# First attention of a two-block transformer kernel: filling parts moved from its ninth phase to its compressed scores, low halves read from PSUM

## The chip, the cores and the metric

The kernel runs on one core of one Trainium2 chip. The metric is the device time of one execution in microseconds; the time of a kernel is the median of its runs. Five engines work side by side and meet only at semaphores: TensorE (PE in the profile; its weight loads are PEld), VectorE (DVE), ScalarE (ACT), GpSimd (POOL) and SyncE (SP), which issues the weight loads from memory. Each engine takes its own instructions strictly in their order.

## The reference

Two transformer blocks over 512 tokens of width 1024, in float32. The part around the change is the first block's attention (native sparse attention), in which 8 query heads in 2 groups of 64 channels look at compressed keys, selected blocks and a window:

```python
kc = compress(kv[0], cmp_pos_k[i], w_cmp_k1[i], w_cmp_k2[i])     # 31 compressed keys per group
vc = compress(kv[1], cmp_pos_v[i], w_cmp_v1[i], w_cmp_v2[i])
lc = jnp.einsum('bghqd,bgcd->bghqc', qb, kc)
pc = masked_softmax(lc, cmp_end[None, :] <= t[:, None])
o_c = jnp.einsum('bghqc,bgcd->bghqd', pc.astype(vc.dtype), vc)
...
o = gates[0] * o_c + gates[1] * o_s + gates[2] * o_w
y_a = o @ w_o_nsa[i]
c = causal_dwconv(c_val * jax.nn.sigmoid(c_gate), conv_w[i], conv_b[i])
c = jax.nn.silu(layernorm(c, conv_ln_g[i], conv_ln_b[i]))
y_b = c @ w_conv_out[i] + b_conv_out[i]
h = h + (ga * y_a + gb * y_b) @ w_out[i]
```

With 512 tokens there are 8 blocks of 64 keys, all of which are selected, so that both the selected and the window branch are causal attention over all earlier tokens, with keys and values of their own. The depthwise convolution has 31 taps over 512 channels, and the layernorm behind it takes its mean over these channels.

## The kernel before

Every float32 operand of TensorE is split into a high and a low half (`_hi`, `_lo`), and a product is three matmuls: high by high, low by high, high by low. A **unit** is one output tile of 128x512 accumulated over 8 blocks of 128 channels; a **part** is one eighth of it, three matmuls of 512 columns (L519 to L521). Weights come in slots of 128x1024: ScalarE makes `w_hi` (L1855) and GpSimd `w_lo` (L472). The high half of anything else is a copy on ScalarE (L1844), the low half a subtraction on VectorE (L1149).

The first attention stands between 124 and 343 us. It works on four pairs of heads. It has nine **phases** of four steps each, one step per query block (`j` and `i` in the code count them from 0; the text counts phases and steps from the first, pairs from 0 as the code does). The first, third, fifth and seventh phase make a pair's scores against the selected keys, the second, fourth, sixth and eighth those against the window's, and each phase turns and uses the probabilities of the phase before it: `turn` transposes a block of keys (L725), ScalarE and VectorE split it (`pt_hi`, `pt_lo`), `values` multiplies it with the values (L733). So the ninth phase has no scores, only transposes and values. Before the first phase and at the end of the second, fourth and sixth `cmp_scores(p)` makes the scores against the 31 compressed keys: two mask matmuls (L752) and 24 matmuls of 32 columns (L758).

Between these pieces TensorE does parts of 19 other units, the **filling parts**: three further query tiles and the 16 tiles of the merge gates, 152 parts. Their places are written out by hand in `NSA_FILL`: per step the parts after the scores, the parts at the step's end, and in the third, fifth, seventh and ninth phase a third number for the parts between the transposes and the values of the compressed branch. `nsa_made(j, i)` adds the table up; by it ScalarE and VectorE know in which step they scale or convert for a finished unit (`nsa_evict`). Eight parts stand outside the table behind it.

VectorE also does the 124 convolution taps (`taps`, L1206 and L1209): `EARLY_TAPS` of them before the attention, the others one or two a step until none is left. `LN_ADD` names the steps in which the finished channels are added up for the layernorm's mean; the ninth phase starts with a matmul of that sum (L816). Before the attention the compressed keys and values come out of PSUM bank 4 and 5 into `kc_f` and `vc_f`, ScalarE makes their high halves and VectorE their low ones:

```python
dve.tensor_copy(kc_f[0:HD, 0:NC1], ps[0:HD, 4, 0:NC1]).then_inc(s_cmp["out"], 1)
dve.tensor_copy(kc_f[HD:P, 0:NC1], ps[HD:P, 4, NC1:2 * NC1]).then_inc(s_cmp["out"], 1)
dve.tensor_tensor(vc_f[:], ps[0:2 * NC1, 5, 0:P], own[:], ALU.mult).then_inc(s_cmp["out"], 1)
...
low(kc_lo[:], kc_f[:], kc_hi[:], s_cmp["klo"])
low(vc_lo[:], vc_f[:], vc_hi[:], s_cmp["klo"])
```

TensorE waits for both (`s_cmp["klo"]`) before `cmp_scores(0)`.

## Time and profile before

| What | Value |
|---|---|
| Runs | 2183.87, 2184.62, 2186.61 us; median 2184.62 |
| Profiled execution | 2185.68 us, its span 2183.9 us |
| Mean granted TensorE clock | 0.994 of full speed |
| TensorE matmuls | busy 2146.1 us, 98% of the span, 10192 instructions |
| Weight loads of TensorE | busy 81% |
| VectorE, ScalarE, GpSimd | busy 46%, 40%, 43% |
| Chain that ended last | TensorE 89%, VectorE 6%, ScalarE 3%, nothing that the profile shows 1% |
| `w_hi` on ScalarE | 352 times, 1058 ns each |
| `w_lo` on GpSimd | 352 times, 2424 ns each |
| Part's three matmuls (128x512) | 391 to 399 ns each from start to end, overlapping |

A row of a timeline gives start, duration, engine, line, operation, output and inputs, and in square brackets how long the engine was idle before it and for whom. Matmuls are pipelined: their durations overlap, and what one costs is the distance from start to start. The kernel is one stream of matmuls with few gaps; other engines matter where TensorE waits for them.

### The profile page before, as it was taken

The page shows a single profiled execution, that of the slowest core. Times are in us where ns is not written, and L with a number is a line of the kernel's source. Part 1 is how long each engine was busy: PE and PEld are TensorE (multiplying, and loading weights), DVE is VectorE, ACT ScalarE, POOL GpSimd, SP SyncE. Part 2 cuts the span into 40 slices and gives each one's busy share as a digit, 9 for nine tenths or more (in the row PEclk, how much of TensorE's full clock was granted, in tenths as well). Part 3 has the DMA queues.
Part 4 walks back from the last instruction along what each step waited for, and adds up shares of the span by engine and source line. Part 5 has one row for each costly group of instructions (what it writes and reads, how often), then busy time and mean ns, then how long its engine had stood idle before and what let it go on. Part 6 is the DMA issues. An engine that isn't in the chain of part 4 may idle for free.

```text
span 2183.9 us, 25305 instructions
## 1 busy us (share of the span) xinstructions
PE 2146.1 (98%) x10192; PEld 1758.8 (81%) x10192; DVE 1013.6 (46%) x1637; ACT 869.6 (40%) x1358; POOL 933.8 (43%) x424
## 2 busy tenths in 40 slices
PE   9999999999999999999999999999999999999998
PEld 7877778888888887777778888888888888888886
...
DMA packets 53829, 193.27 MB, mean 88 GB/s; under 512 B 6096, under 2 KB 6224, under 8 KB 53712
## 3 DMA queue, kind: packets, MB, share of 16 engines
...
## 4 chain that ended last, share of the span: by engine, by line
PE 89%; DVE 6%; ACT 3%; issue 1%; DMA 0%; POOL 0%; DVEq 0%; ACTq 0%; POOLq 0%
PE ps L519 27%; PE ps L521 27%; PE ps L520 27%; PE ps L733 1%; DVE ps L1209 1%; PE ps L982 1%; PE ps L713 1%; PE ps L1000 1%; PE ps L725 1%; ACT w_hi L1855 1%; PE ps L615 1%; DVE xg_lo L1169 1%; PE ps L1007 0%; DVE ps L1730 0%; PE ps L715 0%
## 5 line engine op out<-in xcount | busy, mean ns | idle before, releaser
L472 POOL TENSOR_TENSOR w_lo<-w_raw,w_hi 128x1024 fp32r<-128x1024 f32 x352 | 852.6, 2424 | 1211.4 <-ACT w_hi L1855 1211.3
L519 PE MATMUL ps<-xg_hi,w_hi 128*128 128x512 f32 x1688 | 674.1, 399 | 5.4 <-POOL w_lo L486 2.8
L521 PE MATMUL ps<-xg_hi,w_lo 128*128 128x512 f32 x1688 | 661.2, 392 | 0.0
L520 PE MATMUL ps<-xg_lo,w_hi 128*128 128x512 f32 x1688 | 660.7, 391 | 0.0
L1855 ACT ACTIVATE w_hi<-w_raw 128x1024 fp32r<-128x1024 f32 x352 | 372.3, 1058 | 626.5 <-PE ps L521 623.8
L519 PEld LDWEIGHTS ps<-xg_hi,w_hi 128*128 128x128 f32 x1688 | 318.8, 189 | 69.3 <-issue 3.0
L521 PEld LDWEIGHTS ps<-xg_hi,w_lo 128*128 128x128 f32 x1688 | 318.5, 189 | 67.9
L520 PEld LDWEIGHTS ps<-xg_lo,w_hi 128*128 128x128 f32 x1688 | 319.2, 189 | 59.4
L521 PE MATMUL ps<-h_hi,w_lo 128*128 128x512 f32 x688 | 267.8, 389 | 0.0
L519 PE MATMUL ps<-h_hi,w_hi 128*128 128x512 f32 x688 | 267.8, 389 | 0.0
L520 PE MATMUL ps<-h_lo,w_hi 128*128 128x512 f32 x688 | 267.8, 389 | 0.0
L1143 DVE TENSOR_TENSOR ps<-ps,inv_rms 128x512 f32<-128x512 f32 x164 | 113.6, 696 | 194.2 <-PE ps L521 181.1
L521 PEld LDWEIGHTS ps<-h_hi,w_lo 128*128 128x128 f32 x688 | 129.2, 188 | 26.9
L520 PEld LDWEIGHTS ps<-h_lo,w_hi 128*128 128x128 f32 x688 | 129.2, 188 | 26.7
L519 PEld LDWEIGHTS ps<-h_hi,w_hi 128*128 128x128 f32 x688 | 129.2, 188 | 26.6
L1499 DVE TENSOR_TENSOR mixed<-mixed,ps 128x512 f32<-128x512 f32 x48 | 33.0, 688 | 199.9 <-PE ps L521 199.9
L1169 DVE SCALAR_TENSOR_TENSOR xg_lo<-resid,vec,xg_hi 128x512 fp32r<-128x512 f32 x72 | 85.5, 1191 | 12.7 <-ACT xg_hi L1881 12.5
L1209 DVE SCALAR_TENSOR_TENSOR ps<-glu,vec,ps 128x512 f32<-128x512 f32 x116 | 87.1, 751 | 1.9
L1844 ACT ACTIVATE h_hi<-ps 128x512 fp32r<-128x512 f32 x86 | 51.5, 598 | 90.1 <-DVE ps L1761 48.8
L1881 ACT ACTIVATE xg_hi<-resid,vec 128x512 fp32r<-128x512 f32 x72 | 51.7, 717 | 62.7 <-DVE resid L1499 40.2
L481 POOL TENSOR_TENSOR sq_sum<-sq_sum,sq 128x512 f32<-128x512 f32 x42 | 66.2, 1577 | 23.7 <-ACT sq L1878 21.4
L1761 DVE TENSOR_TENSOR ps<-tile_b,ps 128x512 f32<-128x512 f32 x64 | 44.6, 696 | 57.7 <-ACT tile_b L2296 57.7
...
## 6 DMA issues: line engine op xcount, KB each, us to landing
w_raw<-in_weights SPq DMA_DIRECT2D x352, 512.0 KB, 3.5
...
```

The costliest lines, as they stand in the source:

```text
L472: pool.tensor_tensor(w_lo[:, slot, :], w_raw[:, u % RAW, :], w_hi[:, slot, :].bitcast(F32), ALU.subtract).then_inc(w_ready, 1)
L481: pool.tensor_tensor(sq_sum[:], sq_sum[:], sq[:, m % 2:m % 2 + 1, :], ALU.add).then_inc(summed, 1)
L519: pe.matmul(o, w, x, start=start, stop=False)
L520: pe.matmul(o, w, xl, start=False, stop=False)
L521: return pe.matmul(o, wl, x, start=False, stop=stop)
L1143: dve.tensor_tensor(out, ps[:, BANK[u]:BANK[u] + 1, :], R[:], ALU.mult).then_inc(done, 1)
L1169: dve.scalar_tensor_tensor(xg_lo[:, m:m + 1, :], X[:, m:m + 1, :], g, xg_hi[:, m:m + 1, :].bitcast(F32), ALU.mult, ALU.subtract).then_inc( ...
L1209: ins = dve.scalar_tensor_tensor(acc if k < CONV_TAPS - 1 else conv_acc[:, ct, :], src, w, acc, ALU.mult, ALU.add)
L1761: dve.tensor_tensor(t, T2[:, m % 2:m % 2 + 1, :], t, ALU.mult).then_inc(s_mlp["s"], 1)
L1844: act.activation(out, x, ACT.Copy, scale=scale).then_inc(done, 1)
L1855: act.activation(w_hi[:, u % RING, :], w_raw[:, u % RAW, :], ACT.Copy).then_inc(w_hi_ready, 1)
L1881: act.activation(xg_hi[:, m:m + 1, :], X[:, m:m + 1, :], ACT.Copy, scale=g).then_inc(prep_hi, 1)
```

## The change

- `NSA_FILL` and three calls: three parts stand before TensorE's waits for the compressed halves, one inside `cmp_scores(0)`, between the second and the third query block, and two behind it; one part stands inside each later `cmp_scores`. The first phase thus holds 20 parts for 16, the second, fourth and sixth 17, the ninth 9 for 16.
- VectorE makes 64 taps before the attention (62 before), then one a step in the first phase and two a step in the second to the eighth; `cmp_normalise` moves in the first phase from its second step to its fourth; the first sum of channels moves from the first phase's second step to the third phase's third.
- `kc_f` and `vc_f` are gone. The product with `own` is written back into PSUM; high and low halves are made from PSUM, those of the keys in two pieces of 64x31. Two tiny instructions put zeros in the last column of `kc_hi` and `kc_lo` in place of the memset of `kc_f`.

```diff
--- before.py
+++ after.py
@@ -164,10 +164,11 @@
 
 
 MIX_CONV = {0: 2, 1: 3, 4: 5}
-EARLY_TAPS = 62
+EARLY_TAPS = 64
 EARLY_IDLE = 8
-LN_ADD = ((0, 1), (4, 0), (7, 3))
-NSA_FILL = [((2, 2),) * 4] + [((2, 2),) * 4, ((2, 2, 2), (2, 1), (2, 2), (2, 1))] * 4
+LN_ADD = ((2, 2), (4, 0), (7, 3))
+NSA_FILL = [((6, 2), (2, 2), (2, 2), (2, 2))] + [((2, 2), (2, 2), (2, 2), (2, 2, 1)), ((2, 2, 2), (2, 1), (2, 2), (2, 1))] * 3 + [
+    ((2, 2), (2, 2), (2, 2), (2, 2, 0)), ((2, 1, 1), (1, 1), (1, 1), (1, 0))]
 
 
 def nsa_made(j, i):
@@ -276,10 +277,8 @@
             kk_lo = sb("kk_lo", [P, 2, S], F32R, att)
             vv_hi = sb("vv_hi", [P, 2, 2, QB, P], F32R, att)
             vv_lo = sb("vv_lo", [P, 2, 2, QB, P], F32R, att)
-            kc_f = sb("kc_f", [P, NCP], scope=att)
             kc_hi = sb("kc_hi", [P, NCP], F32R, att)
             kc_lo = sb("kc_lo", [P, NCP], F32R, att)
-            vc_f = sb("vc_f", [2 * NC1, P], scope=att)
             vc_hi = sb("vc_hi", [2 * NC1, P], F32R, att)
             vc_lo = sb("vc_lo", [2 * NC1, P], F32R, att)
             gates = sb("gates", [P, QB, 32], scope=att)
@@ -743,7 +742,7 @@
                     part(u0 + at // DC, at % DC, at % DC + 1)
                 made[0] += n
 
-            def cmp_scores(p):
+            def cmp_scores(p, between):
 
                 pe.wait_ge(bank_free, query_unit(p) + 1)
                 if p:
@@ -757,6 +756,8 @@
                             rows = slice(hd * HD, (hd + 1) * HD)
                             mm = pe.matmul(ps[:, 2 + hd, qi * NCP:(qi + 1) * NCP], q[rows, p % 2, qs], k[rows, :],
                                            start=False, stop=t == 2 and qi == QB - 1)
+                    if qi < QB - 1 and between[qi]:
+                        fill(between[qi])
                 mm.then_inc(s_cs["scores"], 1)
 
             def cmp_turn(p):
@@ -793,18 +794,19 @@
                     pe.wait_ge(A1["olo"], b // 2)
                 head_values(A1, event(b) + kb, kb, vv_hi[:, :, b % 2], vv_lo[:, :, b % 2], b % 2 == 0 and kb == 0, b % 2 == 1 and kb == QB - 1)
 
+            fill(3)
             pe.wait_ge(c_act, 5)
             pe.wait_ge(s_kv["lo"], 6)
             pe.wait_ge(s_kv["zero"], 4)
-            pe.wait_ge(s_cmp["klo"], 2)
+            pe.wait_ge(s_cmp["klo"], 4)
             for j in range(9):
                 b = j - 1
                 for i in range(QB):
                     pieces = NSA_FILL[j][i]
                     if j < 8:
                         if j == 0 and i == 0:
-                            cmp_scores(0)
-                            fill(pieces[0])
+                            cmp_scores(0, (0, 1, 0))
+                            fill(2)
                         scores(j, i)
                     if j or i:
                         fill(pieces[0])
@@ -825,7 +827,9 @@
                                 cmp_values(b // 2)
                         turn(b, i)
                     if j % 2 and i == QB - 1 and j < 7:
-                        cmp_scores(j // 2 + 1)
+                        cmp_scores(j // 2 + 1, (0, pieces[2], 0))
+                    elif j == 7 and i == QB - 1:
+                        fill(pieces[2])
                     fill(pieces[1])
             fill(4)
             values(7, QB - 1)
@@ -1261,7 +1265,8 @@
                 dve.wait_ge(unit_done, uu + 1)
                 dve.tensor_tensor(kv_dup[0:HD, j, :], ps[0:HD, BANK[uu], :], R[0:HD, 0, :], ALU.mult).then_inc(s_cmp["dup"], 1)
                 dve.tensor_tensor(kv_dup[HD:P, j, 0:S - 1], ps[HD:P, BANK[uu], 1:S], R[HD:P, 0, 1:S], ALU.mult).then_inc(bank_free, 1)
-            dve.memset(kc_f[:], 0.0).then_inc(s_cmp["out"], 1)
+            for t in (kc_hi, kc_lo):
+                dve.tensor_scalar(t[:, NC1:NCP], ones[:, 0:1], 0.0, None, ALU.mult).then_inc(s_cmp["out"], 1)
             dve.wait_ge(s_cmp["dup"], 4)
             dve.wait_ge(bank_free, U["cmp_in"] + 4)
             blocks(0, "pos_k")
@@ -1303,15 +1308,14 @@
             query_low(0)
             values_low(1)
             dve.wait_ge(unit_done, U["cmp_out"] + 1)
-            dve.wait_ge(s_cmp["out"], 1)
-            dve.tensor_copy(kc_f[0:HD, 0:NC1], ps[0:HD, 4, 0:NC1]).then_inc(s_cmp["out"], 1)
-            dve.tensor_copy(kc_f[HD:P, 0:NC1], ps[HD:P, 4, NC1:2 * NC1]).then_inc(s_cmp["out"], 1)
-            dve.tensor_tensor(vc_f[:], ps[0:2 * NC1, 5, 0:P], own[:], ALU.mult).then_inc(s_cmp["out"], 1)
+            dve.tensor_tensor(ps[0:2 * NC1, 5, 0:P], ps[0:2 * NC1, 5, 0:P], own[:], ALU.mult).then_inc(s_cmp["out"], 1)
             dve.memset(token[:, 12:13], 0.0).then_inc(bank_free, 1)
             dve.wait_ge(s_cmp["khi"], 2)
-            dve.wait_ge(s_cmp["out"], 4)
-            low(kc_lo[:], kc_f[:], kc_hi[:], s_cmp["klo"])
-            low(vc_lo[:], vc_f[:], vc_hi[:], s_cmp["klo"])
+            for g in range(2):
+                rows = slice(g * HD, (g + 1) * HD)
+                low(kc_lo[rows, 0:NC1], ps[rows, 4, g * NC1:(g + 1) * NC1], kc_hi[rows, 0:NC1], s_cmp["klo"])
+            dve.wait_ge(s_cmp["khi"], 3)
+            dve.tensor_tensor(vc_lo[:], ps[0:2 * NC1, 5, 0:P], vc_hi[:].bitcast(F32), ALU.subtract).then_inc(s_cmp["klo"], 2)
             dve.wait_ge(s_kv["lo"], 2)
             scaled(U["gates"], T[:, 0:1, :])
 
@@ -1435,9 +1439,9 @@
                             dve.tensor_copy(gates[:], ps[:, 4, 0:QB * 32].rearrange("p (a b) -> p a b", b=32)).then_inc(s_gate["ready"], 1)
                             dve.wait_ge(s_gate["ready"], 1)
                     nsa_evict(nsa_made(j, i - 1) if i else nsa_made(j - 1, QB - 1) if j else 0)
-                    if tapped[0] < CT * CONV_TAPS:
+                    if j and tapped[0] < CT * CONV_TAPS:
                         taps(1)
-                    if i == 1 and br == 0 and j < 8:
+                    if i == (1 if j else QB - 1) and br == 0 and j < 8:
                         cmp_normalise(p)
                     if j < 8:
                         head_normalise(A1, QB * j + i, i, stat, (prob_s, prob_w)[br],
@@ -1979,9 +1983,12 @@
             query_high(0)
             values_high(1)
             highs(U["cmp_out"] + 1 + RING)
-            act.wait_ge(s_cmp["out"], 4)
-            copy_hi(kc_hi[:], kc_f[:], s_cmp["khi"])
-            copy_hi(vc_hi[:], vc_f[:], s_cmp["khi"])
+            act.wait_ge(unit_done, U["cmp_out"] + 1)
+            for g in range(2):
+                rows = slice(g * HD, (g + 1) * HD)
+                copy_hi(kc_hi[rows, 0:NC1], ps[rows, 4, g * NC1:(g + 1) * NC1], s_cmp["khi"])
+            act.wait_ge(s_cmp["out"], 3)
+            copy_hi(vc_hi[:], ps[0:2 * NC1, 5, 0:P], s_cmp["khi"])
             highs(U["gates"] + 1 + RING)
             taken(U["gates"])
             act.activation(ln_sum[:], T[:, 0, :], ACT.Sigmoid).then_inc(s_gate["sig"], 1)
```

**TensorE, at the first compressed scores.** `cmp_mask_r` is the mask, `kc` the compressed keys, `xg` the normed input of the filling parts. Before:

```order
L520 MATMUL ps<-xg_lo,w_hi 128x512
L521 MATMUL ps<-xg_hi,w_lo 128x512
L752 MATMUL ps<-cmp_mask_r,ident_r 128x128 x2
L758 MATMUL ps<-kc_hi,q_hi 128x32 x2
L758 MATMUL ps<-kc_lo,q_hi 128x32 x2
L758 MATMUL ps<-kc_hi,q_lo 128x32 x2
L758 MATMUL ps<-kc_hi,q_hi 128x32 x2
L758 MATMUL ps<-kc_lo,q_hi 128x32 x2
L758 MATMUL ps<-kc_hi,q_lo 128x32 x2
L758 MATMUL ps<-kc_hi,q_hi 128x32 x2
L758 MATMUL ps<-kc_lo,q_hi 128x32 x2
```

After (the two rows ahead of the mask end the three new filling parts):

```order
L519 MATMUL ps<-xg_lo,w_hi 128x512
L520 MATMUL ps<-xg_hi,w_lo 128x512
L751 MATMUL ps<-cmp_mask_r,ident_r 128x128 x2
L757 MATMUL ps<-kc_hi,q_hi 128x32 x2
L757 MATMUL ps<-kc_lo,q_hi 128x32 x2
L757 MATMUL ps<-kc_hi,q_lo 128x32 x2
L757 MATMUL ps<-kc_hi,q_hi 128x32 x2
L757 MATMUL ps<-kc_lo,q_hi 128x32 x2
L757 MATMUL ps<-kc_hi,q_lo 128x32 x2
L518 MATMUL ps<-xg_hi,w_hi 128x512
L519 MATMUL ps<-xg_lo,w_hi 128x512
L520 MATMUL ps<-xg_hi,w_lo 128x512
```

The first query blocks' small matmuls now stand between filling parts; before, all 24 stood in a row behind the gates' unit, whose rows read like filling parts.

**VectorE, from the query's scaling to the gates' scaling**, ahead of the same scores. `vv` are values, `token` a one-column dummy. Before:

```order
L1143 TENSOR_TENSOR ps<-ps,inv_rms 128x512
L1297 SCALAR_TENSOR_TENSOR q_lo<-ps,q_hi 128x512
L1149 TENSOR_TENSOR vv_lo<-ps,vv_hi 128x4x64 x2
L1307 COPY kc_f<-ps 64x31
L1308 COPY kc_f<-ps 64x31
L1309 TENSOR_TENSOR vc_f<-ps,own 62x128
L1310 MEMSET token 128x1
L1149 TENSOR_TENSOR kc_lo<-kc_f,kc_hi 128x32
L1149 TENSOR_TENSOR vc_lo<-vc_f,vc_hi 62x128
L1143 TENSOR_TENSOR tile_a<-ps,inv_rms 128x512
```

After:

```order
L1213 SCALAR_TENSOR_TENSOR ps<-glu,vec,ps 128x512
L1147 TENSOR_TENSOR ps<-ps,inv_rms 128x512
L1302 SCALAR_TENSOR_TENSOR q_lo<-ps,q_hi 128x512
L1153 TENSOR_TENSOR vv_lo<-ps,vv_hi 128x4x64 x2
L1311 TENSOR_TENSOR ps<-ps,own 62x128
L1312 MEMSET token 128x1
L1153 TENSOR_TENSOR kc_lo<-ps,kc_hi 64x31 x2
L1318 TENSOR_TENSOR vc_lo<-ps,vc_hi 62x128
L1147 TENSOR_TENSOR tile_a<-ps,inv_rms 128x512
L1382 TENSOR_REDUCE c_stat<-ps 128x8
```

The copies into `kc_f` are gone, the product stays in `ps`, and the low halves read `ps`.

**Ninth phase, TensorE between the second transposes and their values.** Before:

```order
L725 MATMUL ps<-ident,prob_w 128x128 x6
L519 MATMUL ps<-xg_hi,w_hi 128x512
L520 MATMUL ps<-xg_lo,w_hi 128x512
L521 MATMUL ps<-xg_hi,w_lo 128x512
L519 MATMUL ps<-xg_hi,w_hi 128x512
L520 MATMUL ps<-xg_lo,w_hi 128x512
L521 MATMUL ps<-xg_hi,w_lo 128x512
L519 MATMUL ps<-xg_hi,w_hi 128x512
L520 MATMUL ps<-xg_lo,w_hi 128x512
L521 MATMUL ps<-xg_hi,w_lo 128x512
L733 MATMUL ps<-pt_hi,vv_hi 128x384
```

After:

```order
L724 MATMUL ps<-ident,prob_w 128x128 x6
L518 MATMUL ps<-xg_hi,w_hi 128x512
L519 MATMUL ps<-xg_lo,w_hi 128x512
L520 MATMUL ps<-xg_hi,w_lo 128x512
L518 MATMUL ps<-xg_hi,w_hi 128x512
L519 MATMUL ps<-xg_lo,w_hi 128x512
L520 MATMUL ps<-xg_hi,w_lo 128x512
L732 MATMUL ps<-pt_hi,vv_hi 128x384
```

One of three parts is gone here. **ScalarE in the same phase**, from the compressed branch's high half to the sigmoids (`sq` are the layernorm's squares). Before:

```order
L1855 ACTIVATE w_hi<-w_raw 128x1024
L1844 ACTIVATE pt_hi<-ps 62x512
L1844 ACTIVATE pt_hi<-ps 128x1024
L2060 ACTIVATE sq<-conv_acc 128x512 x2
L1844 ACTIVATE pt_hi<-ps 128x2x384
L2060 ACTIVATE sq<-conv_acc 128x512 x2
L1855 ACTIVATE w_hi<-w_raw 128x1024
L1844 ACTIVATE pt_hi<-ps 128x2x256
L2037 ACT_TABLE_LOAD
```

After:

```order
L1859 ACTIVATE w_hi<-w_raw 128x1024
L1848 ACTIVATE pt_hi<-ps 128x2x128
L1848 ACTIVATE pt_hi<-ps 62x512
L1848 ACTIVATE pt_hi<-ps 128x1024
L2067 ACTIVATE sq<-conv_acc 128x512 x2
L1859 ACTIVATE w_hi<-w_raw 128x1024
L1848 ACTIVATE pt_hi<-ps 128x2x384
L2067 ACTIVATE sq<-conv_acc 128x512 x2
L1848 ACTIVATE pt_hi<-ps 128x2x256
```

Each `w_hi` stands one step earlier: the first ahead of the small high halves, the second ahead of the high half of 128x2x384 instead of behind it.

## Rows read from the trace of the kernel before

**Rows 1.** Waits of TensorE, 40 to 350 us: total us, times, longest us.
```profile
PE ps L752 <- DVE vc_lo L1149: 4.1, 1, 4.1
PE ps L752 <- ACT prob_w L2001: 1.6, 3, 0.5
PE ps L713 <- ACT prob_s L2001: 0.7, 2, 0.4
```

**Rows 2.** Windows: us, PE, PEld, DVE, ACT, POOL busy (count), clock, DMA share, GB/s.
```profile
128.00:142.00 14.00, 14.00 (x70) 10.84 (x69) 6.20 (x17) 4.15 (x11) 0.00 (x0) 0.63 0.10 40
170.00:177.00 7.00, 6.48 (x46) 5.02 (x45) 3.12 (x8) 1.48 (x6) 0.00 (x0) 0.76 0.15 55
219.00:226.00 7.00, 6.55 (x57) 5.62 (x57) 5.16 (x13) 2.74 (x9) 0.00 (x0) 1.00 0.09 32
266.00:273.00 7.00, 6.51 (x44) 5.20 (x45) 3.68 (x10) 1.22 (x5) 0.00 (x0) 0.76 0.09 35
500.00:790.00 290.00, 290.00 (x1281) 240.24 (x1280) 118.92 (x168) 106.19 (x135) 132.54 (x55) 1.00 0.31 100
```

**Rows 3.** Timeline of TensorE: first mask, two filling parts slow, and two at full clock.
```profile
127.83 0.41 PE L752 MATMUL ps<-cmp_mask_r,ident_r 128*128 128x128 f32 x2 [4.06 <-DVE vc_lo L1149]
...
130.74 0.79 PE L519 MATMUL ps<-xg_hi,w_hi 128*128 128x512 f32 x1
...
133.59 0.47 PE L713 MATMUL ps<-kk_hi,q_hi 64*128 64x128 f32 x2
...
221.23 0.50 PE L519 MATMUL ps<-xg_hi,w_hi 128*128 128x512 f32 x1
...
222.81 0.33 PE L713 MATMUL ps<-kk_hi,q_hi 64*128 64x128 f32 x2
```

**Rows 4.** Timeline of VectorE before the first mask.
```profile
115.25 3.92 DVE L1209 SCALAR_TENSOR_TENSOR ps<-glu,vec,ps 128x512 f32<-128x512 f32 x5
...
122.93 0.28 DVE L1309 TENSOR_TENSOR vc_f<-ps,own 62x128 f32<-62x128 f32 x1
...
123.71 1.48 DVE L1149 TENSOR_TENSOR kc_lo<-kc_f,kc_hi 128x32 fp32r<-128x32 f32 x1 [0.49 <-ACT vc_hi L1844]
125.11 2.47 DVE L1149 TENSOR_TENSOR vc_lo<-vc_f,vc_hi 62x128 fp32r<-62x128 f32 x1
```

**Rows 5.** Timeline of GpSimd, the same stretch.
```profile
122.77 4.67 POOL L472 TENSOR_TENSOR w_lo<-w_raw,w_hi 128x1024 fp32r<-128x1024 f32 x2 [2.34 <-ACT w_hi L1855]
```

**Rows 6.** Timelines of VectorE, ScalarE and TensorE, end of the third phase.
```profile
195.84 1.23 DVE L1339 TENSOR_REDUCE stat<-ps 128x2 f32<-128x1024 f32 x1
...
197.78 0.68 ACT L2001 ACTIVATE prob_s<-ps,stat 128x512 f32<-128x512 f32 x1
...
198.80 0.33 PE L713 MATMUL ps<-kk_hi,q_hi 64*128 64x128 f32 x2
```

**Rows 7.** Timeline of VectorE, end of the eighth phase: the last sum for the mean.
```profile
316.28 0.68 DVE L1415 TENSOR_TENSOR ln_sum<-ln_sum,conv_acc 128x512 f32<-128x512 f32 x1
```

**Rows 8.** Timeline of TensorE, ninth phase: eight transposes, then each step's first values.
```profile
321.49 1.09 PE L725 MATMUL ps<-ident,prob_w 128*128 128x128 f32 x8
...
325.17 0.40 PE L733 MATMUL ps<-pt_hi,vv_hi 128*128 128x512 f32 x1
...
329.27 0.43 PE L733 MATMUL ps<-pt_hi,vv_hi 128*128 128x384 f32 x1
...
333.60 0.28 PE L733 MATMUL ps<-pt_hi,vv_hi 128*128 128x256 f32 x1
...
338.30 0.33 PE L733 MATMUL ps<-pt_hi,vv_hi 128*128 128x128 f32 x1 [0.17 <-DVE pt_lo L1149]
```

**Rows 9.** Timeline of VectorE, ninth phase: low half of the eight transposes.
```profile
323.68 1.22 DVE L1149 TENSOR_TENSOR pt_lo<-ps,pt_hi 128x1024 fp32r<-128x1024 f32 x1 [3.13 <-ACT pt_hi L1844]
```

**Rows 10.** Timeline of ScalarE, ninth phase: the two sigmoids.
```profile
333.81 3.72 ACT L2037 ACTIVATE merge<-merge 128x2048 f32<-128x2048 f32 x2
```

**Rows 11.** Timeline of TensorE behind the last values of the second attention.
```profile
1114.78 0.79 PE L519 MATMUL ps<-fo_hi,w_hi 128*128 128x512 f32 x1 [1.41 <-DVE fo_lo L1149]
```

## The prediction

> **What bounds the kernel now.** I read the waits of TensorE first. The page's table says that TensorE is busy nearly all of the span, so that only three things can change the time: waits of TensorE, stretches in which it runs at a lower clock, and work taken from it. The change takes no work from TensorE (the same filling parts, elsewhere), so the first two are the whole account. The waits view of the stretch 40 to 350 us [rows 1] shows where the first attention waits: 4.1 us once, before the mask that opens the scores against the compressed keys, for VectorE's `vc_lo`; 0.7 us in two waits for `prob_s` in the first phase; 1.6 us in three waits for `prob_w` (0.52 each, before the compressed scores of the pairs 1 to 3). Then the granted clock by windows [rows 2]: 0.63 over the 14 us behind the long wait, that is 14 x 0.37 = 5.2 us of clock lost; 0.76 over 7 us at 170 and again at 266 us (1.7 us each), both right behind a 0.52 us wait and the 24 matmuls of 32 columns; and 1.00 at 219 us, where the same instructions stand behind the same wait. The two levels of the clock are 2.4 and 1.2 GHz: two filling parts took 1.58 us at the one and 2.85 us at the other [rows 3], a ratio of 1.8 where the clock's is 2. So of lost clock I count 0.92: 4.8 us in front, 1.6 us for each later fall.
>
> The third view is VectorE's timeline before the long wait [rows 4]: `kc_lo`, 128x32, took 1.48 us and `vc_lo`, 62x128, took 2.47 us, while the product `vc_f`, as small but read from PSUM, took 0.28. GpSimd ran two `w_lo` from 122.77 to 127.44 us [rows 5]; these two low halves read both operands from SBUF and the second ends within 0.2 us of GpSimd's. They waited for GpSimd, not for arithmetic.
>
> **The change, part by part.**
>
> *Low halves from PSUM.* The two copies into `kc_f` go (0.43 us up to the product's start), `kc_lo` becomes two short pieces and `vc_lo` one, all with one operand in PSUM. Two more taps stand ahead: five took 3.92 us, so 1.57 us [rows 4]. VectorE's product moves from 122.93 to 122.93 - 0.43 + 1.57 = 124.07 us and ends at 124.3. From the product's end to `kc_lo` it took 0.55 us before over ScalarE's high halves; ScalarE no longer waits for VectorE with `kc_hi`, so this is a bound from above: 124.85. Then 0.2 + 0.2 + 0.28 = 0.7 us give 125.5 in place of 127.6. The bounds: if the pieces cost nothing 124.9, if one of them still waits for a `w_lo` (end at 125.1 or 127.4) 127.6. I take 125.5, since every PSUM operand beside that `w_lo` ran at its short time.
>
> The Trainium skill, page "VectorE: DVE Perf Modes", section "Rules for kernel authors", advises for elementwise work on a matmul's output to accept the PSUM rate or "copy PSUM→SBUF first if you'll do many ops", which is what the kernel before does. By that rule the change would lose here; by the rows above it gains, since the copied operands were those that took long.
>
> *Three parts before the scores.* TensorE was done with the gates' unit at 127.83 - 4.06 = 123.8 us [rows 3]. A part is three matmuls of 512 columns; 1281 of mostly such matmuls took 290 us [rows 2], 0.226 each, so 0.68 a part. Three parts last until 125.8, just past 125.5. The wait of 4.1 us shrinks to about 0.1: **-4.0**. These parts need the weights of the first pair unit, converted long before. What was late next is TensorE's own queue.
>
> *The clock in front.* With no idle ahead of it and a part between the second and the third query block's small matmuls, the stretch starts at full clock: **-4.8**, between 0 (it falls all the same) and -5.2.
>
> *VectorE's first phase.* Four taps, one running sum and the compressed normalisation leave its first two steps. Its peaks then come as the scores do, and the two waits for `prob_s` go: **-0.7**. The last step carries the normalisation, 1.5 us more, but TensorE's next scores wait for the exponentials of the step's scores, which precede it.
>
> *One part inside the compressed scores of pairs 1 to 3.* It stands behind the 0.52 us wait and covers none of it, so its only worth is the clock. The same rows fell at two places and not at a third, so one part may or may not tip it. I take one of the two falls as gone, **-1.6**, between -3.2 and +1.6 (a fall at the third place too).
>
> *The counts shift.* With four more parts in the first phase, units end one step earlier or later afterwards, and so do the scaling on VectorE (0.69) and the `w_hi` on ScalarE (1.06). In the third phase VectorE's second step now holds a `merge` scaling and its third the moved sum into `ln_sum`: the peak of the fourth query block moves from 195.84 to about 196.6 us. ScalarE's exponentials ended at 198.46 and TensorE's next scores began at 198.80 without a wait [rows 6]; the slack of 0.3 is less than the shift, so a wait of some 0.6 appears. In the seventh phase a scaling and a `w_hi` in its third step do the same for 0.5. **+1.1**, between 0 (TensorE's other work hides it) and +2.
>
> *The ninth phase.* It loses seven of 16 parts, 4.8 us of work. Was it cover? First, the mean's matmul waits for the third sum into `ln_sum`. Before, the last tap fell a step earlier; now tap and sum stand at the end of the eighth phase. The sum ran at 316.28 for 0.68 us [rows 7] and the tap adds 0.78, with a `w_hi` on ScalarE ahead of the high half: the matmul that stood at 317.0 starts 0.9 us later. Then the chain transposes, high half on ScalarE, low half on VectorE, values. The eight transposes began at 321.49 and their values at 325.17 [rows 8]; the low half between them ran from 323.68 for 1.22 us [rows 9], so the values could have begun at 324.95: slack 0.2, where two parts (1.4 us) go. At the following values, 329.27, slack is nil. The last ones, at 338.30, waited 0.17 us, because ScalarE was in the two sigmoids of 128x2048 (3.72 us from 333.81) [rows 10]. The steps between values were 4.10, 4.33 and 4.70 us. Without the parts they are set by the chain: 4.6 (a `w_hi` now comes before the high half), 3.2 (that `w_hi` of 1.06 us is gone from here) and 5.0 (table load, sigmoids, high and low half in a row). So the phase ends 0.2 + 1.1 - 0.5 - 0.3 = 0.5 us sooner than before from a start 0.9 us late: with 4.8 us of work gone it is 0.4 us longer, and **+5.2** is what the parts taken away cost here as idle. Bounds +4.2 and +6.2.
>
> *The clock in the ninth phase.* Its end is now 1.4 us idle, six matmuls of 128 columns and four of one column. The nearest row is at 1114.78 us: a wait of 1.41 us behind small matmuls, and the next 512-column matmul takes 0.79 us, as long as the one at 130.74 and not 0.50 like the one at 221.23, so the clock is at its lower level [rows 3, 11]. I take one fall, priced like those at 170 and 266 us before the 0.92: **+1.7**, between 0 and +3.4.
>
> The Trainium skill, page "TensorE: Matmul & The Clock Gate", section "Why this matters for your kernels", says that it takes a long gap between bursts of matmuls to lose the clock. By that rule none of the ninth phase's short waits would cost a fall; the falls at 170 and 266 us, behind 0.52 us, contradict it. It is the first rival below.
>
> Sum: -4.0 - 4.8 - 0.7 - 1.6 + 1.1 + 5.2 + 1.7 = -3.1. The profiled execution took 2185.68 us (its span 2183.9 and 1.8 around it) and would come to 2182.6; it stands 1.06 above the median of the three runs, and from that median of 2184.62 the forecast is 2181.5.
>
> **The rivals.**
>
> *The clock holds in the ninth phase.* The waits there are split by full matmuls, unlike at 1114 us. Then the last term is 0: -4.8, 2179.8; with both later falls gone too -6.4, 2178.2. For it: 219 us, no fall. Against: both sides of the last wait are small matmuls.
>
> *More is late behind.* All three places fall, or ScalarE's and VectorE's shifted work adds waits elsewhere: 1.6 to 4 us on top, -1.5 to +1, 2183.1 to 2185.6.
>
> *The front doesn't do what it says.* `vc_lo` comes at 127 us after all, TensorE idles 1 us and the clock falls as before: -3.1 + 4.8 + 1.0 = +2.7, 2187.3. Against: the PSUM rows.
>
> *The ninth phase at half clock, slower than before.* From the transposes at 321.49 to the values at 338.30 stand 16.8 us; less 0.2 idle and six parts (4.1) 12.5 us of work remain. At half clock they take 12.5 x 1.8 = 22.5, which passes the chain's 16.3 by 6.2; the tail behind adds 1.7. With -4.8 for the rest and the later falls kept (+1.6): +4.7, 2189.3. It decides only if the clock falls at the first of the waits and stays down until the end, for some 17 us; half of that would end at no change. The long slow stretch in front lasted 10 us and had far less work in it.
>
> **How the numbers follow.** Forecast case 0.38; the clock holds in the ninth phase 0.36, nearly all of it below 2180.25; more is late 0.14; the front fails 0.05; the ninth phase at half clock 0.05; the rest, 0.02, lies on both sides. What a measurement of this kernel tells from no change is about 0.2%, 4.4 us: faster means below 2180.25, slower above 2189.0. So faster 0.35 (the first rival without its upper edge), same 0.59, slower 0.06. The range that holds 8 in 10 runs from the better end of the first rival with a little measured spread, 2177.7, to the worse end of the second, 2185.5.
>
> **What would show it.** Right: no wait before the first mask above 0.3 us; clock 1.00 from 128 to 142 us; `kc_lo` and `vc_lo` at or below 0.3 us; waits of 0.9, 1.0, 1.2, 1.3, 0.4 and 1.4 us in the ninth phase, 5 to 6 us in all; waits of half a microsecond at the fourth phase's and the eighth's first scores; a slow stretch behind the ninth phase's last values. Wrong: ninth-phase waits of under 4 us (then a link of the chain that I took as fixed was itself driven by TensorE), a wait for `vc_lo`, or a clock that differs from this at the four places.

## The result, and the profile after

The changed kernel took 2195.30 us (median of 6 runs, 2191.54 to 2196.53) against 2186.05 for the kernel before in the same comparison: a ratio of 1.0042 with a 95% interval of 1.0032 to 1.0053, 9.2 us slower. I had forecast 2181.5 with a range up to 2185.5, and slower than before with a chance of 0.06. The forecast was wrong, in sign and by more than its range.

The profiled execution took 2196.53 us, its span 2194.8 (before 2183.9). The waits of TensorE, 40 to 360 us, which answer to [rows 1] (total us, times, longest us; line numbers are those of each kernel's own file):

```profile
PE ps L732 <- DVE pt_lo L1153: 7.5, 7, 1.8
PE ps L712 <- ACT prob_s L2008: 1.9, 3, 0.9
PE ps L818 <- DVE ln_sum L1419: 1.7, 1, 1.7
PE ps L751 <- ACT prob_w L2008: 1.6, 3, 0.5
PE ps L724 <- DVE prob_s L1351: 1.4, 1, 1.4
PE ps L772 <- DVE pt_lo L1153: 0.7, 1, 0.7
```

The wait of 4.1 us for `vc_lo` is gone, as forecast. But 6.6 us of waits (those of [rows 1] and the 0.2 of [rows 8]) have become 14.8. The windows, which answer to [rows 2] (us, busy us and count of PE, PEld, DVE, ACT and POOL, granted clock, DMA share, GB/s):

```profile
128.00:142.00 14.00, 14.00 (x85) 10.16 (x84) 8.74 (x20) 6.62 (x17) 4.15 (x2) 1.00 0.32 96
170.00:177.00 7.00, 7.00 (x35) 5.41 (x34) 2.67 (x7) 1.82 (x6) 0.00 (x0) 0.77 0.22 75
217.00:228.00 11.00, 10.48 (x70) 8.30 (x69) 6.08 (x14) 3.98 (x12) 2.44 (x1) 0.84 0.15 49
345.00:360.00 15.00, 14.37 (x67) 12.15 (x68) 7.19 (x13) 11.20 (x16) 4.78 (x2) 0.89 0.22 70
```

In front the clock is 1.00 for 0.63. Of the two later falls, at 170 and 266 us, the second is gone (1.00 from 262 to 275 us, where its mask now stands), and there is one at 222 us that was not there before. The one I expected behind the ninth phase is there. In front, the low halves read from PSUM are short although two `w_lo` run beside them (start us, us, engine, line, operation):

```profile
125.03 4.72 POOL L471 TENSOR_TENSOR w_lo<-w_raw,w_hi 128x1024 fp32r<-128x1024 f32 x2 [3.98 <-ACT w_hi L1859]
...
125.26 0.41 DVE L1153 TENSOR_TENSOR kc_lo<-ps,kc_hi 64x31 fp32r<-64x31 f32 x2 [0.17 <-ACT kc_hi L1848]
...
125.70 0.28 DVE L1318 TENSOR_TENSOR vc_lo<-ps,vc_hi 62x128 fp32r<-62x128 f32 x1
```

To see where the time goes I cut the attention at the four masks that open the compressed keys' scores, at the mean's matmul and at the matmul that spreads the normalisation behind the ninth phase. TensorE by these stages (us, busy us and count, granted clock, DMA share, GB/s), the kernel before:

```profile
127.83:170.94 43.11, 41.91 (x222) 0.88 0.15 49
170.94:219.45 48.51, 47.96 (x281) 0.96 0.13 45
219.45:266.49 47.04, 46.46 (x282) 1.00 0.13 45
266.49:317.02 50.53, 50.51 (x294) 0.97 0.15 44
317.02:342.74 25.72, 25.55 (x134) 1.00 0.13 41
```

and the changed kernel:

```profile
126.29:166.67 40.38, 38.48 (x227) 1.00 0.21 66
166.67:218.50 51.83, 49.29 (x284) 0.97 0.13 41
218.50:270.33 51.83, 49.22 (x284) 0.97 0.14 42
270.33:324.38 54.05, 50.50 (x296) 1.00 0.13 40
324.38:351.64 27.26, 23.07 (x112) 0.94 0.13 39
```

By the second mask the changed kernel is 4.3 us ahead; the three stages behind it lose 3.3, 4.8 and 3.5 us, though each has one filling part (three matmuls, 0.7 us) more. The ninth phase, 22 recorded matmuls shorter, takes 1.5 us longer. At its end the kernel is 8.9 us behind, of the 10.9 between the two spans and the 9.2 between the medians. The other 2.0 us come later, where the change edits nothing: the clock of this execution also falls at 1080, 1120 and 1760 us (0.83, 0.83 and 0.86 over 10 us each), that of the kernel before only at 1110 us (0.83). Within the attention, then, the middle stages lost what I had not priced. Their waits on TensorE's timeline (start us, us, in brackets the idle time before and who ended it):

```profile
148.82 1.09 PE L724 MATMUL ps<-ident,prob_s 128*128 128x128 f32 x8 [1.37 <-DVE prob_s L1351]
...
189.44 0.44 PE L732 MATMUL ps<-pt_hi,vv_hi 128*128 128x384 f32 x1 [1.14 <-DVE pt_lo L1153]
...
241.93 0.44 PE L732 MATMUL ps<-pt_hi,vv_hi 128*128 128x384 f32 x1 [1.79 <-DVE pt_lo L1153]
```

with a fourth of 1.08 us in the seventh phase. Ahead of each, VectorE and GpSimd (start us, us, engine, line, operation):

```profile
145.71 3.06 DVE L1351 TENSOR_SCALAR prob_s<-prob_s,stat,gates 128x512 f32<-128x512 f32 x2
...
146.09 2.39 POOL L471 TENSOR_TENSOR w_lo<-w_raw,w_hi 128x1024 fp32r<-128x1024 f32 x1 [6.49 <-ACT w_hi L1859]
...
184.99 2.41 POOL L471 TENSOR_TENSOR w_lo<-w_raw,w_hi 128x1024 fp32r<-128x1024 f32 x1 [14.99 <-ACT w_hi L1859]
...
185.16 2.51 DVE L1399 TENSOR_TENSOR prob_c<-prob_c,c_stat 128x248 f32<-128x248 f32 x1
```

The scaling of `prob_c` takes 2.51 us, and ends 0.27 us behind a `w_lo` that began 0.17 us before it. So do the other two in the fifth and seventh phase; only the one of the first phase is short. In the kernel before, the four of them took 0.42 each (duration ns min/median/max, first line the changed kernel, second the kernel before):

```profile
L1399 DVE TENSOR_TENSOR prob_c<-prob_c,c_stat x4: 416/2497/2506, 145.2 to 287.3; 128x248 f32<-128x248 f32 x4
...
L1395 DVE TENSOR_TENSOR prob_c<-prob_c,c_stat x4: 416/416/419, 141.9 to 283.4; 128x248 f32<-128x248 f32 x4
```

That is the same picture as `kc_lo` and `vc_lo` in front [rows 4, 5], which I had read as waits for GpSimd, and then had not looked for at the places to which the shifted counts move a `w_lo`. The Trainium skill, page "SBUF — State Buffer", section "SBUF: two separate sides", says that VectorE and GpSimd share a pair of ports that is locked for a whole instruction: an operation of VectorE with two SBUF inputs, or in one of its two-port modes, blocks until a GpSimd operation that began first has ended. The rows above agree for `prob_c`, which has two SBUF inputs, and so do the rows of the experiments. `prob_s` has one tensor input and waits as well, 3.06 us for 1.00; which mode it ran in no row shows.

The theory to test, the **collision theory**: the table's shifted counts bring ScalarE's `w_hi`, and with it GpSimd's `w_lo`, one step earlier, beside operations of VectorE that have all their tensors in SBUF. The rival, the **load theory**: VectorE simply has more work in these steps (a merge scaling of 0.68 us that also came one step earlier, the first phase's normalising), and the long duration is only a part of it.

### The profile page after: what moved, and what is told of

The parts are those of the page before. It is cut to its first block, busy times and chain, and to the rows that moved or that the text cites. A ratio compares the mean times of both kernels' runs of the same rounds, so it can differ in the third digit from the quotient of the medians.

```text
span 2194.8 us, 25305 instructions
## 1 busy us (share of the span) xinstructions
PE 2149.2 (98%) x10192; PEld 1758.7 (80%) x10192; DVE 1020.7 (47%) x1637; ACT 870.0 (40%) x1359; POOL 933.9 (43%) x424
## 4 chain that ended last, share of the span: by engine, by line
PE 89%; DVE 6%; ACT 3%; issue 1%; DMA 0%; POOL 0%; DVEq 0%; ACTq 0%; POOLq 0%
PE ps L518 27%; PE ps L520 27%; PE ps L519 27%; PE ps L986 1%; PE ps L1004 1%; PE ps L732 1%; PE ps L712 1%; DVE stat L1343 1%; ACT w_hi L1859 1%; PE ps L614 1%; PE ps L724 1%; DVE xg_lo L1173 1%; PE ps L1011 0%; DVE pt_lo L1153 0%; PE ps L1013 0%
## 5 line engine op out<-in xcount | busy, mean ns | idle before, releaser
L1162 DVE TENSOR_TENSOR sq_sum<-sq_sum,ps 128x512 f32<-128x512 f32 x57 | 39.1, 687 | 69.4 <-ACT ps L1876 69.1
```

Source lines behind the costliest of these rows:

```text
L1162: dve.tensor_tensor(sq_sum[:], sq_sum[:], ps[:, NB:NB + 1, :], ALU.add).then_inc(summed, 2 if m == DC - 2 and in_two_parts(n) else 1)
```

## The experiments

All medians are set against the kernel before on the same chip. Each kernel has one trace, of one execution; executions of one kernel differ in their mean granted clock (0.994 to 0.996 in the six of the changed kernel), so a single fall of the clock that a trace shows need not stand in the others.

| kernel | median, us | before, us | ratio, 95% interval |
|---|---|---|---|
| the change | 2195.30 | 2186.05 | 1.0042 (1.0032 to 1.0053) |
| high_late | 2190.05 | 2186.22 | 1.0020 (1.0010 to 1.0030) |
| scale_late | 2205.72 | 2186.22 | 1.0094 (1.0080 to 1.0108) |
| table_only | 2198.31 | 2186.22 | 1.0060 (1.0047 to 1.0072) |
| vector_only | 2189.46 | 2186.22 | 1.0018 (1.0009 to 1.0027) |
| mean_clear | 2182.82 | 2184.76 | 0.9993 (0.9985 to 1.0002) |
| vector_clear | 2183.95 | 2184.76 | 0.9998 (0.9989 to 1.0007) |
| ninth_thin | 2193.34 | 2184.76 | 1.0032 (1.0019 to 1.0044) |
| front_four | 2179.56 | 2184.76 | 0.9977 (0.9969 to 0.9986) |
| norm_late | 2191.20 | 2185.06 | 1.0030 (1.0020 to 1.0039) |
| part_behind | 2182.86 | 2185.06 | 0.9997 (0.9988 to 1.0006) |
| sum_early | 2178.16 | 2185.06 | 0.9971 (0.9960 to 0.9983) |
| first_thin | 2179.86 | 2185.06 | 0.9976 (0.9967 to 0.9985) |

### high_late: the w_lo back in its old steps

```diff
 # ScalarE; NSA_WAS is NSA_FILL of the kernel before
-                while counted[0] < n // DC:
+                while counted[0] < (n if at_query(counted[0]) or late is None else late) // DC:
...
-                    nsa_evict(nsa_made(j, i - 1) if i else nsa_made(j - 1, QB - 1) if j else 0)
+                    nsa_evict(nsa_made(j, i - 1) if i else nsa_made(j - 1, QB - 1) if j else 0,
+                              nsa_made(j, i - 1, NSA_WAS) if i else nsa_made(j - 1, QB - 1, NSA_WAS) if j else 0)
```

`at_query` picks the three query tiles among the units; they stay on the new counts, the merge tiles go back to the old ones.

> The changed kernel, with ScalarE alone back on the unit counts of before: a weight tile's rounding to w_hi, and so GpSimd's subtraction that makes w_lo from it, again begins in the third step of the odd phases and no longer in the second. Everything else, VectorE's scaling of the finished merge tiles included, stays on the shifted counts. Collision theory (GpSimd's w_lo of 2.4 us holds up VectorE's operations whose operands all lie in SBUF): VectorE's prob_c scaling falls from 2.5 to 0.42 us in the third, fifth and seventh phase, prob_s of the first phase's last step from 3.06 to 1.0 us, the waits of 1.37, 1.14, 1.79 and 1.08 us at TensorE shrink to 0.3 or less, and the time falls by 5 to 7 us against the changed kernel's 2195.3, to about 2189.5. Load theory (VectorE has simply too much in these steps: merge scaling and normalising together): the same waits, and 2195 +-1.

It came out 5.2 us faster than the changed kernel, at the near end of the forecast. The scaling of `prob_c`, and TensorE's waits:

```profile
L1406 DVE TENSOR_TENSOR prob_c<-prob_c,c_stat x4: 416/416/419, 144.2 to 280.5; 128x248 f32<-128x248 f32 x4
```

```profile
PE ps L739 <- DVE pt_lo L1160: 3.4, 4, 1.1
PE ps L825 <- DVE ln_sum L1426: 1.9, 1, 1.9
PE ps L719 <- ACT prob_s L2015: 1.9, 2, 1.2
```

All four waits of the middle stages are gone; the four for `pt_lo` that are left lie in the ninth phase. VectorE's merge scaling was in the same step as in the changed kernel, so its load there was not the cause by itself. Waits for `prob_s` at the third and fifth phase's end, and the mean's, are left.

### norm_late: the w_lo stays, the operation that it holds up goes elsewhere

```diff
-                    if i == (1 if j else QB - 1) and br == 0 and j < 8:
+                    if i == (2 if j else QB - 1) and br == 0 and j < 8:
                         cmp_normalise(p)
```

> The changed kernel, ScalarE's and GpSimd's work and all counts as they are; only VectorE's normalising of the compressed probabilities moves from the second to the third step of the odd phases, out of the way of the w_lo that stands in the second. Collision theory: prob_c takes 0.42 instead of 2.5 us, the three waits of 1.14, 1.79 and 1.08 us at TensorE go (the first phase's 1.37 and the mean's 1.72 stay), unless the third step, now 1.4 us fuller, makes others of some tenths: 3 to 4.5 us faster than the changed kernel's 2195.3, about 2191.5. Load theory: the same 1.4 us of small operations only move, and new waits of about a microsecond appear in the third step: 2195.

4.1 us faster than the changed kernel (3.1 when each is set against the kernel before in its own comparison): within the forecast, though nothing on ScalarE or GpSimd was moved. All four `prob_c` take 0.42 us, and the waits of 1.14, 1.79 and 1.08 us are gone. In the third phase the `w_lo` at 182.33 us now meets VectorE's low half and tap, which take one operand from PSUM, and neither is longer for it (before, 0.96 and 0.75 as well):

```profile
182.33 2.40 POOL L471 TENSOR_TENSOR w_lo<-w_raw,w_hi 128x1024 fp32r<-128x1024 f32 x1 [13.48 <-ACT w_hi L1859]
...
183.31 0.96 DVE L1153 TENSOR_TENSOR pt_lo<-ps,pt_hi 128x768 fp32r<-128x768 f32 x1 [0.96 <-ACT pt_hi L1848]
184.18 0.75 DVE L1213 SCALAR_TENSOR_TENSOR ps<-glu,vec,ps 128x512 f32<-128x512 f32 x1
```

In the third and fifth phase the 1.4 us of small operations did not turn into a wait in the third step. In the seventh there is one, and it is a collision again: a later `w_lo` meets `prob_s` (two of 128x384, 0.87 us otherwise), TensorE waits 0.74 us for the low half behind it and 1.38 us, for 0.73, at the phase's end.

```profile
284.95 2.62 POOL L471 TENSOR_TENSOR w_lo<-w_raw,w_hi 128x1024 fp32r<-128x1024 f32 x1 [3.42 <-ACT w_hi L1859]
...
285.44 2.74 DVE L1351 TENSOR_SCALAR prob_s<-prob_s,stat,gates 128x384 f32<-128x384 f32 x2
...
288.83 0.39 PE L732 MATMUL ps<-pt_hi,vv_hi 128*128 128x256 f32 x1 [0.74 <-DVE pt_lo L1153]
```

So 4.0 us of waits went and 1.0 came: 3.0 us net, and the clock falls behind that last wait (0.83 from 290 to 300 us) and no longer at the masks.

### scale_late: the merge scaling back, the w_lo stays

The same edit as high_late, in VectorE's loop in place of ScalarE's.

> The changed kernel, with VectorE alone back on the unit counts of before: its scaling of a merge tile (0.68 us) leaves the second step of the odd phases for the third, while ScalarE's w_hi and GpSimd's w_lo stay in the second. Load theory: each of the three waits in the odd phases falls by up to 0.7 us, about 2 us in all, to 2193. Collision theory: the w_lo still begins beside the prob_c scaling, which starts 0.6 us earlier and ends with the w_lo as before; waits and time stay, 2195 +-1 (a bank that comes free later could add some tenths).

Both expectations missed: the kernel is 10 us slower than the changed one. The first line of its waits says why, and it is a cost of the experiment's own: the filling parts wait for banks whose merge tiles are scaled too late.

```profile
PE ps L525 <- DVE merge L1154: 14.5, 7, 4.1
```

So its time tells nothing between the theories. Its trace does. With the 0.68 us of scaling out of the step, `prob_c` gets in ahead of the `w_lo` and takes 0.42; the operation behind it, `prob_s` (two of 128x256, 0.73 us otherwise), is held up in its place:

```profile
286.86 0.42 DVE L1406 TENSOR_TENSOR prob_c<-prob_c,c_stat 128x248 f32<-128x248 f32 x1
...
287.29 2.38 POOL L478 TENSOR_TENSOR w_lo<-w_raw,w_hi 128x1024 fp32r<-128x1024 f32 x1 [14.19 <-ACT w_hi L1867]
...
287.39 2.75 DVE L1358 TENSOR_SCALAR prob_s<-prob_s,stat,gates 128x256 f32<-128x256 f32 x2
```

Which operation pays was a matter of tenths of a microsecond here; an operation with only SBUF operands in the 2.4 us of the `w_lo` paid in both kernels.

### table_only and vector_only: the change in two halves

table_only is the kernel before with the edits to TensorE's order alone (`NSA_FILL`, the three parts in front, `between`); vector_only the kernel before with all the rest of the diff.

> The kernel before, with only what the change does to TensorE's order: three parts ahead of the first scores' waits, parts between the compressed keys' scores, the new table; VectorE and ScalarE as before (fp32 copies kc_f and vc_f, taps, first phase's normalising, additions in their old steps), but on the shifted unit counts. Collision theory: most of the loss is here; the first phase's prob_c scaling stands in its second step, away from a w_lo, so that the 3.06 us is gone, but the three 2.5 us are there: front gain of 4 to 6, less 4 to 5 of ninth phase, less 4 of collisions and their followers, less clock: about +5 to +8 against before, near 2192. If instead VectorE's own changes cost the time (taps out of the first phase, normalising in its fourth step): about 2183 to 2187 here.

> The kernel before, with only the edits to VectorE and ScalarE: low halves from PSUM, two taps earlier, no taps in the first phase, its normalising in the fourth step, the first addition in the third phase; TensorE's order and the unit counts as before. Collision theory: no collision in the odd phases; the front wait of 4.1 falls by some 1.6 us, the first phase's two waits of 0.7 us go: 2 to 3 us faster than before, 2183.5. If VectorE's own changes cost the time: 2188 or more.

table_only lost 12 us, more than the whole change, and 4 more than the most that I expected. Here the first phase's normalising was still in its second step, and I had thought it clear of a `w_lo` there. It is not: `prob_c` takes 2.5 us four times out of four, and in the first phase TensorE pays all of it.

```profile
L1401 DVE TENSOR_TENSOR prob_c<-prob_c,c_stat x4: 2493/2497/2499, 140.2 to 289.5; 128x248 f32<-128x248 f32 x4
```

```profile
147.00 0.53 PE L714 MATMUL ps<-kk_hi,q_hi 64*128 64x512 f32 x2 [3.12 <-ACT prob_s L2007]
```

Lost clock comes on top: 0.56 from 147 to 150 us, behind that wait, and 0.82 over the ninth phase (0.94 in the changed kernel).

vector_only was meant to gain 2 to 3 us and lost 3.2. (Its first phase has one tap a step left, not none as the expectation says.) Half of it behaved: the wait for `vc_lo` is 1.8 us for 4.1, the first phase's two waits are gone, and no `prob_c` is long. One wait of 0.83 us for `prob_s` came at the third phase's end. A loss that the trace explains sits at the mean. The last tap now falls at the end of the eighth phase, the third sum into `ln_sum` right behind it, and that sum has SBUF operands alone:

```profile
317.46 2.34 POOL L470 TENSOR_TENSOR w_lo<-w_raw,w_hi 128x1024 fp32r<-128x1024 f32 x1 [4.85 <-ACT w_hi L1855]
...
317.55 2.80 DVE L1415 TENSOR_TENSOR ln_sum<-ln_sum,conv_acc 128x512 f32<-128x512 f32 x1
...
320.40 2.08 PE L816 MATMUL ps<-ln_sum,mean_ch 128*128 128x512 f32 x2 [2.76 <-DVE ln_sum L1415]
```

The sum takes 2.80 for 0.68 us [rows 7], the mean's matmul waits 2.76, and it takes 2.08 us where it took 1.12 in the kernels before and after: the clock had fallen (0.94 over that last stage). The wait and that clock are some 4 us, and not the whole of what was lost against the gains in front. In this execution the stages between the second and the fourth mask are 2.6 and 3.1 us longer than in the kernel before, at a clock of 0.93 each for 0.96 and 1.00. Why it fell longer there, no experiment shows; the mean clock of the eleven executions goes from 0.990 to 0.995.

### mean_clear and vector_clear: that w_lo behind the sum

```diff
-                    nsa_evict(nsa_made(j, i - 1) if i else nsa_made(j - 1, QB - 1) if j else 0)
+                    if (j, i) != (8, 0):
+                        nsa_evict(nsa_made(j, i - 1) if i else nsa_made(j - 1, QB - 1) if j else 0)
...
                             cmp_high(b // 2)
+                            if j == 8:
+                                nsa_evict(nsa_made(j, i - 1) if i else nsa_made(j - 1, QB - 1) if j else 0)
```

on ScalarE, in high_late (there with the second limit too) and in vector_only (shown).

> high_late, and behind the eighth phase ScalarE rounds its weight tile only after the compressed values' high half, so that GpSimd's w_lo no longer runs beside VectorE's last addition into ln_sum, for which the mean's matmul waits. Collision theory: the addition takes 0.68 instead of 1.96 us, the mean's wait falls from 1.9 to about 0.7, and the time by 1.3 to 2 us, to 2188.5. Rival (the wait is the late last tap, and the addition's length does not matter): wait and time as in high_late, 2190.

> vector_only with the same edit to ScalarE. Collision theory: the addition falls from 2.80 to 0.68 us, the mean's wait from 2.8 to 0.7 or less, and the half clock on the mean's matmuls behind that wait (2.08 us for two) goes too: 3 to 4 us, to about 2186, the level of the kernel before or a little under it. Rival: VectorE's edits cost elsewhere (the later last tap, the waits at the third phase's first scores): 2189 stays.

In both the sum takes 0.69 us and the mean's wait is 0.65. The gains are 7.2 us between the medians of high_late and mean_clear and 5.5 between those of vector_only and vector_clear (5.8 and 4.0 when each is set against the kernel before of its own comparison). For mean_clear that is much more than the 1.3 to 2 that I forecast. The traces of high_late and mean_clear show 4.3 us of it by the end of the ninth phase: the shorter wait, and a clock of 1.00 in two stages where high_late had 0.97 (the third) and 0.94 (the ninth phase). Why the clock held there, once in a stage that the edit does not reach, no row says. For high_late the single runs lie 6.7 us apart, for mean_clear 3.1. What is shown of this edit is the sum's 0.69 us and the shorter wait, 1.3 us.

### ninth_thin: the ninth phase's parts as cover

The kernel before with the ninth phase's table of the change, and the seven parts behind it:

```diff
-NSA_FILL = [((2, 2),) * 4] + [((2, 2),) * 4, ((2, 2, 2), (2, 1), (2, 2), (2, 1))] * 4
+NSA_FILL = [((2, 2),) * 4] + [((2, 2),) * 4, ((2, 2, 2), (2, 1), (2, 2), (2, 1))] * 3 + [
+    ((2, 2),) * 4, ((2, 1, 1), (1, 1), (1, 1), (1, 0))]
...
             mm.then_inc(s_ln["var"], 1)
-            fill(4)
+            fill(11)
```

> The kernel before, with nothing but the ninth phase's table of the change: seven of its sixteen parts are taken out and stand behind it, in the second filling ahead of the wait for the normalisation's reciprocal, where TensorE has nothing to wait for. The same parts are computed in all. My term for the ninth phase: 7 x 0.68 = 4.8 us of cover lost, all of it turned to idle, plus 1.7 if the clock falls behind it: +5 to +6.5, to about 2192. If the parts were not needed as cover: 2186. If the gaps pull the clock down in the phase itself: 2196 or more.

8.6 us between the medians, interval 4.2 to 9.6, where I expected 5 to 6.5; the five executions lie in two groups, at 2188 and 2193.5. By the traces its last stage is 32.08 us for 25.72, 6.4 more with the same work. Idle is 4.0 us of that, 0.7 of it before the compressed branch's values:

```profile
PE ps L733 <- DVE pt_lo L1149: 3.5, 3, 2.0
```

```profile
338.00:346.00 8.00, 7.07 (x31) 0.79 0.22 66
```

and the clock, 0.79 over 8 us behind the last values, 1.7. In the trace my two terms for the ninth phase hold: the parts were cover, 4.0 of their full price of 4.8, and the fall comes on top. The 0.7 us that is left is in neither.

### front_four and part_behind: what a part between the compressed scores is worth

front_four is mean_clear with no part in the later phases' compressed scores and twelve in the ninth phase; part_behind is mean_clear with each of the three parts right behind those scores in place of between them.

```diff
-                        cmp_scores(j // 2 + 1, (0, pieces[2], 0))
+                        cmp_scores(j // 2 + 1, (0, 0, 0))
+                        fill(pieces[2])
```

> mean_clear, with only the four parts of the front kept: no part stands between the later phases' compressed scores, and the three parts that stood there are back in the ninth phase, twelve instead of nine. Against mean_clear three parts of cover come back, 2.0 us; the odd phases' first-scores waits change with the counts by some tenths. If the parts between the compressed scores bring nothing: 1.5 to 2.5 faster than mean_clear, 2186.5. If they hold the clock there (1.00 for 0.76 in a stretch of 7 us is 1.7 us each): mean_clear's time or up to 2 us more.

> mean_clear, with each of the three parts that stood between the compressed keys' scores of the later phases now right behind those scores: order alone, all counts equal. If the parts between hold the clock: a granted clock of 0.76 to 0.87 at one or two of these places and 1 to 3 us slower than mean_clear's 2182.8. If the clock there hangs on the waits before the masks and what came before them: equal, 2182.8 +-1.

In the trace of part_behind the clock does not need the part. Over the stretches with the 24 small matmuls:

```profile
164.00:172.00 8.00, 7.47 (x61) 1.00 0.08 33
213.00:221.00 8.00, 7.48 (x61) 1.00 0.10 39
261.00:270.00 9.00, 8.46 (x67) 1.00 0.00 0
```

And a part does not always protect it: in the changed kernel the fall at 222 us begins behind one.

```profile
219.61 0.50 PE L518 MATMUL ps<-xg_hi,w_hi 128*128 128x512 f32 x1
...
220.98 0.36 PE L757 MATMUL ps<-kc_lo,q_hi 64*128 64x32 f32 x2
...
221.48 0.79 PE L518 MATMUL ps<-xg_hi,w_hi 128*128 128x512 f32 x1
```

The medians of part_behind and mean_clear are equal, 2182.86 and 2182.82; its three stages are each 0.3 us shorter by the traces, which I take for the price of breaking the small matmuls up. The single executions leave a doubt: six of the eleven of part_behind had a mean clock of 0.995 or 0.996, up to 2187.20 us, all eleven of mean_clear 0.997 or 0.998, up to 2184.08. Whether the part helps in some executions is therefore open. It is not needed where none stands there or right behind: front_four and sum_early had 0.997 or 0.998 in all of their 17 executions. front_four, which gives three parts of cover back, is 3.3 us faster than mean_clear (I expected 1.5 to 2.5) and 5.2 faster than the kernel before, with an interval that leaves 1 out.

### sum_early and first_thin: what else can be had

```diff
-LN_ADD = ((2, 2), (4, 0), (7, 3))
+LN_ADD = ((2, 0), (4, 0), (7, 3))
```

first_thin also has `((6, 2), (2, 1), (2, 1), (1, 1))` for the first phase and the full sixteen parts in the ninth.

> front_four, with the first addition into ln_sum moved from the third phase's third step (where the trace of front_four shows it at 1.24 us beside the end of a w_lo, and TensorE waiting 1.20 us for prob_s four microseconds later) to its first step, where VectorE idles 3 us. Collision theory: that wait falls to 0.6 or less, 0.6 to 1.2 us faster than front_four's 2179.56, about 2178.7. If the wait belongs to the shifted counts alone: no change.

> sum_early, with the four parts of the front taken from the rest of the first phase (16 parts in all there again) and the ninth phase full at sixteen. The ninth phase's waits beyond the compressed values' (1.6 us) go; four parts less in the first phase either uncover VectorE there, up to 2.7 us of idle at its scores or first turn, or stay hidden since its taps are gone. If hidden: 1.5 us faster than sum_early, 2177; if not: 1 us slower, 2180, more if the clock falls.

sum_early has the lowest median, 2178.16 us, 6.9 us below the kernel before. The first sum took 1.24 us in front_four beside the end of a `w_lo`, and 0.69 here; the wait that it lengthened went from 1.20 to 0.63 us, as the collision theory had it. The 1.4 us between the two medians is less than the 3.5 between single executions of sum_early. first_thin's median is 1.7 us above sum_early's, though their executions overlap: the ninth phase's waits but the mean's go, but the first phase's scores wait 1.60 us for `prob_s` and the clock falls at two places (0.94 from 142 to 170 us, 0.87 from 262 to 275). By these waits those four parts were cover too. In the trace of sum_early the granted clock is 1.00 in all five stages.

## Why the prediction was wrong

**The counts shift: the step that failed.** I put +1.1 on it, for a merge scaling and a `w_hi` in steps that had some slack. The two waits for `prob_s` that I meant are there, 0.88 and 0.73 us at the third and the seventh phase's end, and a third of 0.29 at the fifth's: 1.9 in all. What the step left out, and so put at nothing, is that a `w_hi` is followed by a `w_lo` of 2.4 us on GpSimd, and that this holds up VectorE. It costs 1.14, 1.79 and 1.08 us in the odd phases and 1.37 behind the first phase: 5.4 us, which make the term +7.3. high_late removes all four from GpSimd's side and gives 5.2 us back; norm_late removes the three of the odd phases from VectorE's side, makes one anew, and gives 4.1 back. I had the mechanism in hand, with rows, for the front, and used it only where the diff spoke of it.

**Low halves, three parts in front, the clock there** (-4.0, -4.8): right. No wait before the first mask, `kc_lo` 0.41 us for both pieces and `vc_lo` 0.28, clock 1.00. The factor of 0.92 on lost clock is not worked out in the prediction: its ratio of 1.8 gives 0.89, which is 0.2 us less here. The Trainium skill's advice that the prediction quotes (page "VectorE: DVE Perf Modes", section "Rules for kernel authors") is to copy out of PSUM first for many operations. For the two operations that read each of these copies it did not pay: beside a `w_lo` the low halves took 1.48 and 2.47 us from the copies.

**VectorE's first phase** (-0.7): the two waits are gone, but the normalisation, moved into the fourth step, put `prob_s` beside a `w_lo`. I had looked only at the next scores, which do not wait for that normalisation; the first transposes do. It also had a good side that I had not seen: in its old step it would have met a `w_lo` as well, at 3.12 us (table_only).

**One part inside the compressed scores** (-1.6): wrong. One fall went and one came, so the clock's sum is nil, and by the traces of mean_clear and part_behind each part costs 0.3 us more there than elsewhere. With the one in front, 1.2 us. That at 219 us the same rows had held the clock was evidence that something else decides, and I read it as a coin to be tipped.

**The ninth phase** (+5.2) **and its clock** (+1.7): right in size, nearly right in parts. Waits of 1.72, 0.70, 0.98, 0.79, 0.64 and 1.08 us stand where I had written 0.9, 1.0, 1.2, 1.3, 0.4 and 1.4: 5.9 for 6.2. The mean's was twice the forecast, by the same omission: its sum took 1.65 us beside a `w_lo`. The clock's is 15 us x 0.11 = 1.65. The fall stands in the changed kernel and in ninth_thin, but not in mean_clear, whose other ninth-phase waits are of the same kind, 0.5 to 1.1 us: the rival in which the clock holds was nearer than this one trace says. Of the traces with nine parts in that phase, those with a wait of 1.7 us or more in it show the fall behind it (this one, high_late, norm_late, table_only, ninth_thin), those with none above 1.1 do not (mean_clear, part_behind, scale_late); no experiment tests whether that decides. The rule of the long gap that the prediction cites from the Trainium skill (page "TensorE: Matmul & The Clock Gate", section "Why this matters for your kernels") does not tell the two apart.

With what was measured in the place of the forecasts, the sum is -4.1 - 4.8 - 0.7 + 1.2 + 7.3 + (5.9 - 0.2) + 1.65 = +6.3. The trace has +8.9 at the end of the ninth phase, of which 0.6 came before the attention. The last 2 us are in no wait of 0.15 us or more; each stage is 0.2 to 0.6 us busier than its parts and its clock account for. It is not that matmuls right behind a wait are long: the eight transposes at 148.82, behind 1.37 us, took 1.09, as did those of [rows 8] without a wait. What these 2 us are stays open.

None of my rivals had this. "More is late behind" had the right place, with 1.6 to 4 us on top in place of some 12, because it was a margin and not a mechanism with a price.
